# Out projection's weights loaded beside attention, tiles of several stages in shared places, and a third place for the Fourier tables

## What is computed

```python
x = layer_norm(x, ln_emb_g, ln_emb_b)
proj = x @ w_in                                  # 1024 -> 512 + 512 + 128 + 128
u, q, k, v = split(proj)
f = real(fft2(ug, axes=(positions, channels), norm='ortho'))      # 4 groups of 128 channels
fourier = einsum('bsgc,gcd->bsgd', f, w_fourier)
scores = q @ k.T / sqrt(64) - slope * dist       # 8 heads, 2 of keys, window of +-128 tokens, a sink logit
probs = exp(scores - m) / (sum(exp(scores - m)) + exp(sink - m))
heads = concatenate([fourier, probs @ v])
x = layer_norm(2 ** 0.25 * x + heads @ w_out, ln_mix_g, ln_mix_b)
h = square(relu(x @ w_ff1))                      # 1024 -> 4096
y = layer_norm(2 ** 0.25 * x + h @ w_ff2, ln_ffn_g, ln_ffn_b)
```

## Time and profile before

| | us |
|---|---|
| median of 3 runs | 2567.06 (2564.68 to 2567.26) |
| the profiled execution: time / span | 2564.25 / 2562.6 |
| PE busy | 2402.4 (94%) in 12192 matmuls |
| DVE / ACT / POOL busy | 1597.0 (62%) / 1094.0 (43%) / 179.4 (7%) |
| granted PE clock, mean | 0.971 |
| stages (start): b, c, d, u, e | 342, 462, 690, 965, 1786 |

### The profile page before, as it was taken

One profiled execution on the slowest core, in us unless ns is written; L12 is line 12 of the kernel. 1 busy time (PEld: TensorE's weight loads), 2 busy tenths in 40 slices (PEclk: granted clock), 3 DMA queues, 4 the chain that ended last, 5 costly groups with the idle time before them and its releaser, 6 DMA issues. The chain is left out here.

```text
span 2562.6 us, 35326 instructions
## 1 busy us (share of the span) xinstructions
PE 2402.4 (94%) x12192; PEld 2097.6 (82%) x12192; DVE 1597.0 (62%) x2220; ACT 1094.0 (43%) x1740; POOL 179.4 (7%) x246
## 2 busy tenths in 40 slices
PE   4999969899799987999999999997999999999998
PEld 3888859799678865888889999997888888888886
DVE  7544156666456567666676666665546577669667
ACT  2111123688611115444455555554433334544442
POOL 1000000222112210000000000000000011001001
PEclk9999979899899998999999999998999999999999
DMA  7665335322345665555577676665876659877974
GB/s 280 252 264 225 125 139 174 91 75 69 115 146 209 245 252 206 211 214 198 228 270 248 231 286 235 247 241 190 273 260 192 195 168 321 263 226 228 320 227 138
DMA packets 217624, 543.04 MB, mean 212 GB/s; under 512 B 21360, under 2 KB 89840, under 8 KB 198064
## 3 DMA queue, kind: packets, MB, share of 16 engines
q1 hardware_dynamic: 200208, 476.92, 53.4%
q0 software_dynamic: 17312, 64.76, 8.1%
HBM read 361.24 MB, written 180.36 MB: 211 GB/s over the span
## 5 line engine op out<-in xcount | busy, mean ns | idle before, releaser
L1794 DVE TENSOR_TENSOR e_lo<-e_raw,e_hi 128x896 fp32r<-128x896 f32 (+1 forms) x336 | 378.6, 1135 | 259.9 <-ACT e_hi L1777 251.8
L1777 ACT CAST e_hi<-e_raw 128x896 fp32r<-128x896 f32 (+1 forms) x336 | 330.4, 983 | 427.2 <-PE e_bank L65 380.5
L63 PE MATMUL e_bank<-e_hi,e_lo 128*128 128x512 f32 x1120 | 436.7, 390 | 15.6 <-DVE e_lo L1794 15.6
L65 PE MATMUL e_bank<-e_hi 128*128 128x512 f32 x1120 | 436.4, 390 | 0.0
L64 PE MATMUL e_bank<-e_lo,e_hi 128*128 128x512 f32 x1120 | 436.4, 390 | 0.0
L63 PE MATMUL u_bank<-u_x_hi,u_wa_lo 128*128 128x384 f32 (+1 forms) x768 | 274.2, 357 | 29.2 <-DVE u_x_first L1414 20.1
L65 PE MATMUL u_bank<-u_x_hi,u_wa_hi 128*128 128x384 f32 (+1 forms) x768 | 272.9, 355 | 0.0
L63 PEld LDWEIGHTS e_bank<-e_hi,e_lo 128*128 128x128 f32 x1120 | 210.7, 188 | 59.7 <-DVE e_lo L1794 15.9
L65 PEld LDWEIGHTS e_bank<-e_hi 128*128 128x128 f32 x1120 | 210.6, 188 | 43.9
L64 PEld LDWEIGHTS e_bank<-e_lo,e_hi 128*128 128x128 f32 x1120 | 210.7, 188 | 43.7
L63 PE MATMUL u_bank<-u_x_hi,u_wb_lo 128*128 128x384 f32 (+1 forms) x576 | 203.9, 354 | 8.3 <-DVE u_x_rest L1414 8.3
(11 more groups left out here) (192 smaller groups left out, 4338.1 us busy)
## 6 DMA issues: line engine op xcount, KB each, us to landing
u_w_raw<-w_ff SPq DMA_DIRECT2D x48, 1024.0 KB, 7.8
e_raw<-s_t SPq DMA_DIRECT2D x192, 256.0 KB, 3.7
e_raw<-s_h SPq DMA_DIRECT2D x224, 192.0 KB, 2.8
e_raw<-w_ff SPq DMA_DIRECT2D x144, 256.0 KB, 3.9
u_w_sum<-s_ws SPq DMA_DIRECT2D x32, 1024.0 KB, 4.8
e_raw<-s_h SPq DMA_DIRECT2D x112, 256.0 KB, 2.8
s_h<-u_h_sum SPq DMA_DIRECT2D x32, 768.0 KB, 7.0
s_h<-u_h SPq DMA_DIRECT2D x96, 192.0 KB, 2.3
```

The lines of the kernel that those rows point to most:

```text
L63: tensor.matmul(out, w_lo, m_hi, start=first, stop=False, skip_group_check=again)
L65: return tensor.matmul(out, w_hi, m_hi, start=False, stop=last, skip_group_check=again)
L1777: act.copy(part(hi, n), part(raw, n)).then_inc(hi_done, 1)
L1794: dve.tensor_tensor(part(lo, n), part(raw, n), part(hi, n).bitcast(F32), ALU.subtract).then_inc(split, 1)
```

## The change

Three things, and one that follows.

1. **Fourier.** A third raw place for tables, `c_vt_raw`, free once the mixing matrices are made (`ab_split`). Table 2 waits for that, tables 3 and 4 for the split of n - 2. `fold` is cut into `fold_once` (the first half and the ends) and `fold_twice`. ACT casts tables 1 and 2 earlier; DVE interleaves single steps of `z_low` and does `fold_once(1)` ahead of table 3.
2. **Out projection.** SP loads all of w_out behind the bias at the start of attend, into a new tile `d_place` of 32 KB per partition. mix_out begins with heads, x, gain and shift only; ACT casts four pieces of w, then the first heads, then the other four, and DVE likewise. The identity of stage `a` is used.
3. **Shared places.** `mixed` is a part of `d_place`; gain, shift and some small tiles are in `c_k_raw`; the MLP's first raw weights are in `c_vt_raw` and `c_q_raw`, and its small tiles in `c_k_raw`.
4. The first stack of tiles therefore stays until the end, and `d`, `u` and `e` are laid on top of it instead of at the bottom.

Where the operands of the matmuls lie (first byte; each k or slot is a whole multiple of 64 bytes on, except in the tables of `b`, whose rows of 2050 floats put each row tile 8 bytes further on modulo 64):

| stage | moving, before | stationary, before | mod 64 | after | mod 64 |
|---|---|---|---|---|---|
| a | xt 179200, 195584 | w 55968, 96928 | 0 / 32 | the same | 0 / 32 |
| b | tables 68320, 101120 | z 183712, 191904 | multiples of 8 / 32 | the same | the same |
| c | ka 68288, kb 88768 | qs 119488 | 0 / 0 | 125632, 146112 / 176832 | 0 / 0 |
| d | w 70336, 103104 | h 144064, 152256 | 0 / 0 | 113376, 146144 / 187104, 195296 | 32 / 32 |
| u | x_hi 57472, x_rest 114816 | wa 155776, 172160; wb 188544, 194688 | 0 / 0 | 80544, 137888 / 178848, 195232; 211616, 217760 | 32 / 32 |
| e | hi 57536, lo 90304 | hi, lo | 0 / 0 | 96992, 129760 | 32 / 32 |

```diff
-        t_raw = k_raw[:].rearrange("p v t -> p (v t)")[:, 0:2 * WIDE].rearrange("p (s w) -> p s w", s=2)
+
+        t_raw = [*(k_raw[:].rearrange("p v t -> p (v t)")[:, s * WIDE:(s + 1) * WIDE] for s in range(2)), vt_raw]
...
-                if n >= 2:
-                    pool.wait_ge(t_split, n - 1)
-                pool.dma_start(table(n)[2], table_ds[job][i * P:(i + 1) * P, :]).then_inc(t_ld[n % 2], 16)
+                if n == 2:
+                    pool.wait_ge(ab_split, 2)
+                elif n > 2:
+                    pool.wait_ge(t_split, n - 2)
+                pool.dma_start(table(n)[2], table_ds[job][i * P:(i + 1) * P, :]).then_inc(t_ld[n % 3], 16)
...
             def fold(n):
+                fold_once(n)
+                fold_twice(n)
+
+            def fold_once(n):
...
+            def fold_twice(n):
+                count = len(units[n][1])
                 dve.drain()
...
             table_low(0)
-            z_low(0, 0)
+            z_low_of(0, 0)
             table_low(1)
-            z_low(0, 1)
+            z_low_of(0, 1)
             table_low(2)
+            z_low_of(0, 2)
+            fold_once(1)
+            z_low_of(0, 3)
             table_low(3)
-            fold(1)
+            fold_twice(1)
             fold_low(1)
...
             table_high(0)
             copy_bias(0)
+            table_high(1)
             z_high(0, 0)
-            table_high(1)
+            table_high(2)
             z_high(0, 1)
-            table_high(2)
             table_high(3)
             fold_high(1)
...
             sp.dma_start(bias[:], bias_d).then_inc(bias_in, 16)
+            load_w_out(sp)
...
-        gain = al.sb("gain", [P, D])
-        shift = al.sb("shift", [P, D])
+        gain, shift, b12 = place2[:, 0:D], place2[:, D:2 * D], place2[:, 2 * D:2 * D + 4 * P]
+        yg = place2[:, 2 * D + 4 * P:4 * D + 4 * P].rearrange("p (s c) -> p s c", s=2)
...
-        mixed = al.sb("mixed", [P, 2, 7, 4 * P])
+        mixed = place[:, 0:2 * 7 * 4 * P].rearrange("p (s j c) -> p s j c", s=2, j=7)
...
-            for k in range(KT):
-                sp.dma_start(w_raw[k], w_out[k * P:(k + 1) * P, :]).then_inc(w_ld[k], 16)
-            sp.dma_start(gain[:], ln_g.partition_broadcast(P)).then_inc(const_in, 16)
-            sp.dma_start(shift[:], ln_b.partition_broadcast(P)).then_inc(const_in, 16)
-            sp.dma_start(ident[:], ident_d).then_inc(const_in, 16)
+            sp.dma_start(gain, ln_g.partition_broadcast(P)).then_inc(const_in, 16)
+            sp.dma_start(shift, ln_b.partition_broadcast(P)).then_inc(const_in, 16)
...
-            split_heads(0)
             for k in range(KT):
+                if k == KT // 2:
+                    split_heads(0)
                 act.wait_ge(w_ld[k], 16)
                 act.copy(w_hi[:, k, :], w_raw[k]).then_inc(w_hi_done, 1)
...
-            rest_of_heads(0)
             for k in range(KT):
+                if k == KT // 2:
+                    rest_of_heads(0)
                 dve.wait_ge(w_hi_done, k + 1)
...
-            pe.wait_ge(const_in, 48)
             for n in range(2, NT):
                 product(n)
                 transpose(n - 2)
...
-        p1 = al.sb("p1", [P, 512])
         u2 = al.sb("u2", [P, 512])
-        u3 = al.sb("u3", [P, 512])
-        c22 = al.sb("c22", [P, 512])
-        h = al.sb("h", [P, 2, 2, 512])
-        h_sum = al.sb("h_sum", [P, 4, 512])
```

More of the change, by code:

```diff
@@ L695, in _, with attend @@
                     channels(n + 1, 1)
-def attend(nc, bias_d, ident, operands, load_queries, heads_d):
+def attend(nc, bias_d, ident, operands, load_queries, heads_d, load_w_out):
     AHEAD = {"scores": 6, "bias": 5, "exp": 4, "turn": 3, "high": 2, "rest": 1, "values": 0}
@@ L1071, in mix_out @@
         heads_v = heads_d.rearrange("(k p) t -> p k t", p=P)
-        w_raw = [*(mixed.rearrange("p s j c -> p (s j c)")[:, k * D:(k + 1) * D] for k in range(KT - 1)), w_last[:]]
+        w_raw = [place[:, k * D:(k + 1) * D] for k in range(KT)]
         block = ctx.enter_context(nc.Block())
@@ L1417, in w_sums @@
             def w_sums(n, s, first=False):
-                raw = w_raw[:, s, :, :]
+                raw = w_raw[s]
                 if not first:
@@ L1971, in build, with load_keys_values, load_queries, load_w_first @@
-    mlp_down(nc, s["x1"], s["h"], d["w_ff2"], s["t"], d["ln_ffn_g"], d["ln_ffn_b"], y)
+        q_raw = ctx.enter_context(nc.sbuf_tensor("c_q_raw", [P, 2, NH, P], F32))
+        with ExitStack() as stages:
+            q_ld = [nc.alloc_semaphore(f"c_q_ld{slot}") for slot in range(2)]
+            q_view = s["proj"][FOUR:KROW, :].rearrange("(h d) t -> d h t", d=HD)
+            def load_keys_values(sp):
+                for g in range(NG):
+                    tok = slice(g * GRP, (g + 1) * GRP)
+                    for half in range(2):
+                        sp.dma_start(k_raw[half * HD:(half + 1) * HD, :, tok],
+                                     s["proj"][KROW:KROW + P, tok].rearrange("(v d) t -> d v t", d=HD)
+                                     ).then_inc(k_ld[g], 16)
+                sp.dma_start(vt_raw[:], s["proj"][VROW:, :]).then_inc(v_ld, 16)
+            def load_queries(pool, b, slot=None):
+                slot = b if slot is None else slot
+                for half in range(2):
+                    pool.dma_start(q_raw[half * HD:(half + 1) * HD, slot, :, :], q_view[:, :, bass.ds(b * P, P)]
+                                   ).then_inc(q_ld[slot], 16)
+            fourier(nc, s["proj"], (chan, wf, in_ld), vt_raw, k_raw, q_raw, [d["table0"], d["table1"]], s["heads"],
+                    load_keys_values, load_queries)
+            x_more = stages.enter_context(nc.sbuf_tensor("u_x_first", [P, 3, 4 * 512], F32))
+            x_first = [x_more[:, j, :] for j in range(3)]
+            keys = k_raw[:].rearrange("p v t -> p (v t)")
+            w_raw = [tile.rearrange("p (b c) -> p b c", b=4) for tile in (
+                vt_raw[:, 0:4 * 512], q_raw[:].rearrange("p s h t -> p (s h t)"))]
+            small = (vt_raw[:, 4 * 512:5 * 512], keys[:, 8 * 512:9 * 512], keys[:, 9 * 512:10 * 512],
+                     keys[:, 4 * 512:8 * 512].rearrange("p (f k c) -> p f k c", f=2, k=2),
+                     keys[:, 0:4 * 512].rearrange("p (b c) -> p b c", b=4))
+            x_ld = [nc.alloc_semaphore(f"u_x_first_ld{j}") for j in range(3)]
+            w_ld = [nc.alloc_semaphore(f"u_w_ld{slot}") for slot in range(2)]
+            w_out_ld = [nc.alloc_semaphore(f"d_w_ld{k}") for k in range(KT)]
+            def load_w_first(sp):
+                for p in range(2):
+                    sp.dma_start(w_raw[p], d["w_ff1"][p * P:(p + 1) * P, :].rearrange("p (b c) -> p b c", b=4)
+                                 ).then_inc(w_ld[p], 16)
+            def load_x_first(pool):
+                for j in range(3):
+                    pool.dma_start(x_first[j].rearrange("p (q c) -> p q c", q=4),
+                                   s["xb"][0:4, :, j, :].rearrange("q p c -> p q c")).then_inc(x_ld[j], 16)
+            with ExitStack() as mixing:
+                place = mixing.enter_context(nc.sbuf_tensor("d_place", [P, KT * D], F32))
+                def load_w_out(sp):
+                    for k in range(KT):
+                        sp.dma_start(place[:, k * D:(k + 1) * D], d["w_out"][k * P:(k + 1) * P, :]
+                                     ).then_inc(w_out_ld[k], 16)
+                attend(nc, d["bias"], ident, (k_raw, vt_raw, q_raw, snk, k_ld, v_ld, q_ld, snk_in), load_queries,
+                       s["heads"], load_w_out)
+                mix_out(nc, s["x_norm"], s["heads"], d["ln_mix_g"], d["ln_mix_b"], ident, place, keys, w_out_ld,
+                        s["x1"], s["xb"], load_x_first, load_w_first)
+            mlp_up(nc, s["xb"], d["w_ff1"], s["ws"], s["h"], (x_first, w_raw, x_ld, w_ld, small))
```

87 lines of the change are left out of this document (26 added, 61 removed).

## The result

| | before | after |
|---|---|---|
| median, us | 2567.16 (2564.68 to 2567.88, 4 runs) | 2550.4 (2549.22 to 2551.67, 4 runs) |
| ratio | | 0.9936 [0.9919, 0.9954] |
| span of the profiled execution | 2562.6 | 2550.0 |

The change makes the kernel 16.8 us faster (0.64%). The forecast was 2594, slower; rival B had 2548.6.

The account below looks back on a forecast made before the run. PE was taken as the bound, busy nearly throughout mlp_up and mlp_down. 2564.25 - 6.2 (Fourier) - 9.4 (mix_out) + 47 (operand place) = 2595.6, taken a little lower as 2594 us; range 2546 to 2606.

Parts of the forecast that it names:

- rival B: Operand place costs nothing in d, u and e, perhaps distance modulo 64 matters; kernel faster, 2548.6 us; chance 0.38.
- where the operands lie, +47 us: In d, u and e, operands moved 32 past a multiple of 64 lengthen matmul steps, costing 47.0 us.
- Place: The forecast's own case: operand place modulo 64 decides in d, u and e; slower, 2578 to 2608 us; chance 0.54.
- 384 columns, 3.4 ns a step: In u, 2688 matmuls of 384 columns each take 3.4 ns longer off a multiple of 64: 9.1 us.
- Fourier, -6.2: At the Fourier stage's start, earlier tables and new DVE order let PE start channels(1) 6.2 us earlier.
- the prediction's upper bound: Fourier stage: gain of 11 us if PE's idle time is short enough that the clock stays up.
- Start of mix_out, -9.4: At mix_out's start, PE begins sooner, waits for no w piece and clocks higher, saving 9.4 us.
- Attend, 0: Loading w_out beside attend costs nothing; up to 5 us lost if queries land behind the weights.

Follow-up runs that it names:

- a_d0: Kernel before with 160 bytes of padding ahead of stage a's moving tiles, moving and stationary operands at the same place modulo 512: 2559.41 us, ratio 0.9974.
- shift32: Kernel before with 32 bytes put under all tiles of d, u and e, nothing else different: 2568.74 us, ratio 1.0003.
- a_x32: Kernel before with 32 bytes of padding ahead of stage a's moving tiles only: 2566.73 us, ratio 0.9994.
- a_w0: Kernel before with 32 bytes of padding ahead of stage a's stationary tiles and 32 ahead of its moving ones: 2567.43 us, ratio 0.9998.
- fourier_only: Kernel before with the changed Fourier stage alone: 2560.41 us, ratio 0.9975.
- no_fourier: Changed kernel with the old Fourier stage, keeping the early w_out load and shared places: 2558.79 us, ratio 0.9968.
- w_late: Changed kernel with w_out loaded at the start of mix_out again, all places and orders as changed: 2556.0 us, ratio 0.9958.

## Why the prediction was wrong

**The step that failed: where the operands lie, +47 us.** It took the one thing that the table of places showed at a glance, 32 past a multiple of 64, for the cause of the 6.7 ns by which a step of a is longer than one of e. The 6.7 ns are real and are due to place: 160 bytes of padding take them away (a_d0). But what counts is the distance between the two operands modulo 256, which is 96 in a and 0 in d, u and e, and the change moves both operands together. By itself the term is 0 (shift32: 1.0003 [0.9994, 1.0012]).

**What the trace had against it.** The prediction listed it itself: the 256-wide steps of b cost nothing though both operands lie off, so "off a multiple of 64" could not be the whole rule. And a, d, u and e split alike by place modulo 64 and by distance, so that they could not tell one from the other. Against rival B stood the claim that in b the steps of 512 columns never settle at 227, "not even where both operands are 32 past". The table of places has no such step: the wide pieces begin 2056 bytes or more into a row, so modulo 64 they lie at 40, 48, 56 and 0 while z lies at 32, and modulo 256 they are 72 to 96 from it. b, too, was slow at distances other than 0 alone, and speaks for the distance. Place was given 0.54; the simplest reading of a correlation was priced above the kernel's worked-out savings.

**Rival B** had the sign, the size (2548.6 against 2550.4) and the idea of the distance. Its "modulo 64" was wrong: a_x32 and a_w0 have distance 0 modulo 64 and stay at 233 ns.

**384 columns, 3.4 ns a step:** at 32 bytes of distance nil, at 128 2.6. Not tested by the change.

**Fourier, -6.2:** right. PE's step on `b_ends_hi` came 6.2 us earlier, as worked out, and the rest of table 3 began at 368.24 on the scale of the execution before against 368.3. By the medians the Fourier change alone saves 6.7 us (fourier_only). The profiled pair has 2.0 us more in the stage, which goes with the clock, as the prediction's upper bound had it: with one wait of 2.26 us in place of 2.87 and 4.06, it was at 0.50 for some 7 us instead of 17. Part of that is the chance of the execution taken before, whose b is the longest of the 14.

**Start of mix_out, -9.4:** 10.4 in the profiled pair, 8.3 by the medians of no_fourier. The heads took 6.9 us (7.7 was used), PE started 2.35 us behind them (2.3), and one slow stretch of 3.2 us at 0.50 was left. Right in sum; the working did not split it between the early load and the new order, and w_late shows that the load is about half. The 6.6 MB given for the loads at the old start are 7.1 by their sizes (eight, two and two of 512 KB, gain and shift of 512 KB, the identity of 64 KB); no term uses the figure.

**Attend, 0:** right for PE, wrong on POOL, whose wait was to be under 1 us and was 9.45. The queries did land among the last of the weights, 10 us after their issue; DVE used them at 477.95 without a wait, 13.5 us after the issue, and attend's matmuls lost nothing (223.64 us with the load in no_fourier, 223.6 before).

The Trainium skill, "SBUF — State Buffer" (section "Who interferes with whom"), gives PE two independent read ports that wait on nobody. The runs differ: moving one of the two operands by 32 bytes lengthens 512-column steps of u from 226.7 to 233.3 ns, moving both by 32 leaves them. Two reads without effect on each other would not show that, though what couples them stays open. The prediction's other figure is less than its section says: in the Trainium skill, "TensorE: Matmul & The Clock Gate" (section "Back-to-back issue gap") gives N/2.4 + 2.5 ns for an isolated matmul, and about 131 ns at 512 columns for a stream with a weight load before each. The 226.7 ns of such a stream here agree with neither.

## What to carry to other kernels

When two stages with the same instruction run at different pace, look for what differs between pairs of operands as well as in each one, and price a guess from such a comparison low until an edit that changes it alone has been timed. In this kernel a stream of matmuls of 512 fp32r columns wants moving and stationary tile a multiple of 256 bytes apart; a pad of 160 bytes in the allocation was enough (7.7 us in a stage of 300). A transfer moved beside an earlier stage is worth what PE still waits for it, and other edits made with it can bring as much (w_late: about half and half), so time it by itself.

## What the runs showed of the hardware

- Distance of the moving from the stationary operand modulo 256, full clock, 512 columns: 0 gives steps of 226.7 ns; 32, 64, 96 and 128 give 232.4 to 233.4 in a and u, 72 to 96 give 233 to 234 in b. At 384 columns 173.3 at 0 and 32, 174.0 at 64, 176.0 at 128. At 256 columns none of it shows (119 in b at 72 to 96, 119 in attend at 0, from the second matmul of a pair to the next).
- In e, where only some of three successive steps are apart, the mean is 228.9 at 128 and 232.2 at 32, where the step L64 has 235.8.
- At the half clock steps of 512 columns take 427 ns in b, whose distances are not 0, and in e, at 0.
